# Latents normed inside the attention stage, head weights in fewer pieces, and the squares of x summed in the output projections

## The reference, cut to what matters

```python
def rms_norm(x, w):
    y = x * rsqrt(mean(x * x, axis=-1) + EPS)
    return y * w

# each layer of the first block; the second block opens alike with norm_mix
h = rms_norm(x, norm_w[l]) * (1.0 + scale) + shift
parts = split_in(h @ w_in[l])          # 256 columns cq, 128 ckv, 32 kr, ...
q = rms_norm(cq, q_norm_w) @ w_uq      # 8 heads of 96; then a norm per head, rope on 32
kv = rms_norm(ckv, kv_norm_w) @ w_ukv  # 8 heads of 64 + 64
...
x = x + gate * (y @ w_out[l])
```

## Time and profile before

| | us |
|---|---|
| median of 3 runs | 4379.31 (4378.44 to 4383.56) |
| the profiled execution: its time | 4386.62 |
| its span | 4384.8 |
| TensorE busy | 3901.9 (89%) |
| VectorE busy | 2111.7 (48%) |
| ScalarE busy | 1575.0 (36%) |
| GpSimd busy | 617.0 (14%) |

### The profile page before, as it was taken

How to read it: one execution, slowest core, us unless ns; L and a number is a source line. 1 busy time by engine, 2 the same in 40 slices (tenths; PEclk the granted TensorE clock), 3 DMA queues, 4 the chain that set the end, 5 groups by cost and what they waited for, 6 DMA issues and landing times. The chain is left out here.

```text
span 4384.8 us, 41863 instructions
## 1 busy us (share of the span) xinstructions
PE 3901.9 (89%) x16132; PEld 2780.2 (63%) x16132; DVE 2111.7 (48%) x2657; ACT 1575.0 (36%) x2450; POOL 617.0 (14%) x300
## 2 busy tenths in 40 slices
PE   4899799999899799999876889898999897999996
PEld 1687555558686455567655866576777675666664
DVE  0391366662373366651438423233343226666665
ACT  1412345541322245441452235522221114555552
POOL 0021200002021200001110011022333330111111
PEclk9999889998999799989888989999999997999997
DMA  4211100002211112122112211022233337999985
GB/s 173 77 39 32 36 15 29 29 29 91 68 44 41 31 53 63 58 80 93 30 20 68 49 40 20 10 72 78 82 94 77 89 121 257 360 352 353 354 293 211
DMA packets 339924, 450.95 MB, mean 103 GB/s; under 512 B 45149, under 2 KB 214418, under 8 KB 338194
## 3 DMA queue, kind: packets, MB, share of 16 engines
q1 hardware_dynamic: 325026, 405.30, 29.5%
q0 software_dynamic: 12112, 25.19, 1.6%
q10 hardware_dynamic: 2592, 17.83, 1.0%
HBM read 408.41 MB, written 59.24 MB: 107 GB/s over the span
## 5 line engine op out<-in xcount | busy, mean ns | idle before, releaser
L1140 PE MATMUL values<-probs,vp 128*128 128x512 f32 x672 | 349.0, 601 | 12.0 <-issue 6.4
L1228 ACT ACTIVATE probs<-scores 128x512 f32<-128x512 f32 (+1 forms) x336 | 196.0, 583 | 307.9 <-PE scores L220 306.2
L218 PE MATMUL scores<-q_hi,k_rest 97*128 97x512 f32 (+1 forms) x336 | 262.4, 781 | 0.0
L3555 PE MATMUL dp<-h_t,abt 128*128 128x512 f32 x544 | 241.9, 597 | 1.1 <-ACT abt L3604 0.9
L3586 ACT ACTIVATE expert_hi<-wu 128x1024 fp32r<-128x1024 f32 x136 | 144.8, 1065 | 250.6 <-PE gp L220 250.6
L1309 DVE TENSOR_REDUCE mx<-made 128x1 f32<-128x640 f32 (+1 forms) x272 | 203.9, 794 | 28.7 <-PE made L1081 27.9
L218 PE MATMUL gates_ps<-x_t_r,ring_r 128*128 128x512 f32 (+1 forms) x560 | 206.2, 368 | 2.6 <-PEq L84 2.6
L218 PE MATMUL smb<-x_t_r,merge_w_r 128*128 128x512 f32 x480 | 195.9, 408 | 13.9 <-POOL merge_w_r L2802 11.1
L730 DVE SCALAR_TENSOR_TENSOR conv_out<-conv_in,vectors,conv_out 128x1295 f32<-128x1295 f32 (+1 forms) x120 | 205.5, 1713 | 4.3
L219 PE MATMUL gates_ps<-h_t_r,ring_hi 128*128 128x512 f32 (+1 forms) x560 | 206.1, 368 | 0.0
L220 PE MATMUL gates_ps<-x_t_r,ring_hi 128*128 128x512 f32 (+1 forms) x560 | 206.0, 368 | 0.0
(11 more groups left out here) (572 smaller groups left out, 9525.9 us busy)
## 6 DMA issues: line engine op xcount, KB each, us to landing
wg<-in_w_gate SPq DMA_DIRECT2D x34, 2048.0 KB, 10.0
wu<-in_w_up SPq DMA_DIRECT2D x34, 2048.0 KB, 11.2
h_t<-in_w_down SPq DMA_DIRECT2D x34, 2048.0 KB, 9.7
ahead_w<-in_w_ada SPq DMA_DIRECT2D x48, 512.0 KB, 3.9
ring_w<-in_w_in SPq DMA_DIRECT2D x44, 512.0 KB, 4.1
mod_w<-in_w_mod ACTq DMA_DIRECT2D x8, 1536.0 KB, 29.2
ahead_w<-in_w_mod SPq DMA_DIRECT2D x24, 512.0 KB, 3.5
out_w<-in_w_out SPq DMA_DIRECT2D x24, 512.0 KB, 4.9
```

The costliest lines, as they stand in the source:

```text
L218: nc.tensor.matmul(out, lhs[1], rhs[0], start=start, stop=False, **kw)
L1140: nc.tensor.matmul(O[b % 2][:, 0:w], vp[g // 2 % 2][:, kb, g % 2 * VD:g % 2 * VD + P], pr[m % 3][:, 0:w], start=kb == 0, stop=kb == nk - 1 ...
L1228: nc.scalar.activation(pr[m % 3][:, 0:w], S[m % 2][:, 0:w], ACT.Exp, scale=scale).then_inc(s.exped, 1)
L3555: m = nc.tensor.matmul(dp[half][:, :], at[:, j, :], wd[u][:, j, half * 512:(half + 1) * 512], start=j == 0, stop=j == FK - 1)
```

## The change

Three things.

1. *Latents.* `latent_norms` is gone. Inside `attention`, the six items (five in layer 1, which has no context queries) follow the order of `made`. Items 0 and 1 are squared, summed, rooted and scaled ahead of the rope of the keys; item n + 2 in step n of head 0. The spread kr goes to other PSUM banks. Scratch lies in the place of x.
2. *Head weights.* Two DMAs for the query weights in place of six, and first in SP's list; GpSimd copies the exchanged rope columns, ahead of its fills, once the DMAs have landed.
3. *Squares.* In both of the first block's output projections ScalarE squares every finished tile of x and VectorE adds the squares over chunks into one tile `summed`, one tile behind its residual. The next wide norm (layer 1, and the delta stage) needs one ones-product per block, and takes all roots at its beginning. The first pair of its weight halves is loaded, rounded and split in the output projection. Layer 0's own wide norm stays.

The core of the diff:

```diff
 def norm_steps(...):
     def sums(pe, i, j):
+        if summed is not None:
+            if j == 0:
+                nc.tensor.matmul(ps[i % 2][:, 0:w], k.ones[:, :], summed[:, t0:t0 + w], start=True, stop=True)
+                    .then_inc(s.summed, 1)
+            return
...
-        for j in range(DK):
-            square(0, j)
-        round_half(nc, ring, act, 0)
+        if summed is None:
+            for j in range(DK):
+                square(0, j)
+        if fresh:
+            round_half(nc, ring, act, 0)
         take_root(0)
-        round_half(nc, ring, act, 1)
+        if summed is not None:
+            for i in range(1, len(blocks)):
+                take_root(i)
...
 def attention(...):
         @block.sync
+            for c in range(2):
+                sp.dma_start(wq[:, c, :, 0:QK], w_uq[:, c, :, :]).then_inc(s.q_in, 16)
+            sp.dma_start(table[NOPE:P, :], a.rope[NOPE:P, :]).then_inc(s.rope_in, 16)
             sp.dma_start(wkv[:, :, :], ...).then_inc(s.k_in, 16)
-            sp.dma_start(table[NOPE:P, :], a.rope[NOPE:P, :]).then_inc(s.rope_in, 16)
-                for c in range(2):
-                    sp.dma_start(wq[:, c, :, 0:QK], w_uq[:, c, :, :]).then_inc(s.q_in, 16)
-                    sp.dma_start(wq[:, c, :, QK:QK + half], w_uq[:, c, :, NOPE + half:QK]).then_inc(s.q_in, 16)
-                    sp.dma_start(wq[:, c, :, QK + half:P], w_uq[:, c, :, NOPE:NOPE + half]).then_inc(s.q_in, 16)
         @block.gpsimd
+            pool.wait_ge(s.q_in, 32)
+            for c in range(2):
+                for to, at in ((QK, NOPE + half), (QK + half, NOPE)):
+                    nc.gpsimd.tensor_scalar(wq[:, c, :, to:to + half], wq[:, c, :, at:at + half], 1.0, None, ALU.mult)
+                        .then_inc(s.turned_q, 1)
         @block.tensor                      # project(g, i)
+                if g == 0:
+                    pe.wait_ge(s.normed, normed_by[i + 1])
+                if g == 0 and kind == "k":
+                    pe.wait_ge(s.k_in, 16)
+                    pe.wait_ge(s.kr_squared, 3)
+                    pe.wait_ge(s.krope_made, 3)
...
+            for i in range(2):
+                sum_latent(i)
             for n in range(NI):
+                if n + 2 < NB:
+                    sum_latent(n + 2)
                 prepare(0, n)
         @block.vector
+            def scale_latent(i):
+                dve.wait_ge(s.lat_rooted, i + 1)
+                for ap, weight in latent(i)[0]:
+                    nc.vector.scalar_tensor_tensor(ap, ap, weight, lat_root[i % 2][:, 0:made[i][2]], ALU.mult, ALU.mult)
+                        .then_inc(s.normed, 1)
+            for i in range(2):
+                scale_latent(i)
...                                        # the rope of the keys
             for n in range(NI):
+                if n + 2 < NB:
+                    scale_latent(n + 2)
                 prepare(0, n)
...
 def project_residual(...):
+                    act.wait_ge(s.added, n + 1)
+                    to = total_sq[:, t0:t0 + w_] if n < nb else sq[n % 2][:, 0:w_]
+                    nc.scalar.activation(to, k.x[:, 2 * g + c, t0:t0 + w_], ACT.Square).then_inc(s.squared, 1)
...
+            def add_square(n):
+                dve.wait_ge(s.squared, n + 1)
+                nc.vector.tensor_tensor(total, total, sq[n % 2][:, 0:w_], ALU.add).then_inc(s.totalled, 1)
...
                     nc.vector.scalar_tensor_tensor(x, ps[t][:, 0:w_], mod[:, gate_at + n, which:which + 1], x, ...)
+                    if ahead and g * per + t > nb:
+                        add_square(g * per + t - 1)
+            if ahead:
+                add_square(n_pairs * per - 1)
```

More of the change, by code:

```diff
@@ L276, in norm_steps @@
     last = len(blocks) - 1
+    summed, fresh = norm.summed, ring.halves == 0
+    sums_each = 1 if summed is not None else DK
     def store(sp):
@@ L365, in norm_tiles @@
 def norm_tiles(nc, es, norm):
-    sq = norm.squares or [es.enter_context(sbuf(nc, f"rm_sq{i}", [P, 512], F32)) for i in range(4)]
-    lg = es.enter_context(sbuf(nc, "rm_log", [P, 512], F32))
-    root = [es.enter_context(sbuf(nc, f"rm_root{i}", [P, 512], F32)) for i in range(2)]
+    sq = norm.squares
+    if norm.summed is None:
+        lg = es.enter_context(sbuf(nc, "rm_log", [P, 512], F32))
+        root = [es.enter_context(sbuf(nc, f"rm_root{i}", [P, 512], F32)) for i in range(2)]
+    else:
+        lg, whole = None, es.enter_context(sbuf(nc, "rm_roots", [P, T1], F32))
+        root = [whole[:, t0:t0 + w] for t0, w, _ in norm.blocks]
     ps = [es.enter_context(psum(nc, f"rm_ps{i}", [P, 512], F32)) for i in range(2)]
@@ L433, in beside_norm @@
             def beside_norm():
-                for j in range(DK):
-                    steps.sums(pe, 0, j)
+                for i in range(1 if norm.summed is None else len(norm.blocks)):
+                    for j in range(DK):
+                        steps.sums(pe, i, j)
                 for i, (t0, w, _) in enumerate(norm.blocks):
@@ L438, in beside_norm @@
                     for j in range(DK):
-                        if i + 1 < len(norm.blocks) and j < DK // 2:
+                        if norm.summed is None and i + 1 < len(norm.blocks) and j < DK // 2:
                             steps.sums(pe, i + 1, 2 * j)
@@ L862, in latents @@
                                       (1, lambda p: cols_of(w_in, C_CKV, p), evac_kv)], blocks, extra=extra)
[L865 to L869, removed]
-    norm_groups(nc, k, items)
 def norm_groups(nc, k, items):
@@ L1006, in attention, with latent @@
         ONCE = 9
+        kr_out = (O[0], O[1], J[:, 2, :])
+        half = ROPE // 2
+        def latent(i):
+            kind, t0, w = made[i]
+            if kind == "q":
+                return [(cq[:, c, t0:t0 + w], col(k, f"q_norm{l}", c)) for c in range(2)], 1.0 / Q_RANK
+            return [(ckv[:, t0:t0 + w], col(k, f"kv_norm{l}"))], 1.0 / KV_RANK
         def squares_of(i):
@@ L1398, in project_residual @@
     total = T1 - first
[L1399 removed]
+    names = "w_in0 w_in1 w_in2 w_in3 x_in0 x_in1 x_in2 x_in3 rounded rest w_rounded w_rest split products added summed biased squared totalled"
     with ExitStack() as es, stage(nc, names) as s, nc.Block() as block:
@@ L1410, in project_residual @@
         early = DK // 2
+        if ahead:
+            ring, ring_columns, total_sq = ahead
+            sq = [es.enter_context(sbuf(nc, f"{name}_sq{i}", [P, 512], F32)) for i in range(2)]
+            assert nc.sbuf_base <= SUMMED_AT and SUMMED_AT + 4 * T1 <= nc.sbuf_top
         def place(g, c):
@@ L1430, in _ @@
                 sp.dma_start(k.x[:, pair, first:T1], kept[:, pair, first:T1]).then_inc(x_in[g], 16)
+            if ahead:
+                for n in range(2):
+                    load_half(sp, ring, n, ring_columns)
         @block.gpsimd
@@ L1442, in _ @@
                                             ALU.subtract).then_inc(s.split, 1)
+            if ahead:
+                for n in range(2):
+                    rest_half(nc, ring, pool, n)
         @block.tensor
@@ L1681, in sum_squares @@
                 last.then_inc(s.qk_summed, 1)
-            for j in range(DK):
-                first.sums(pe, 0, j)
+            for i in range(len(X_NORMS)):
+                first.sums(pe, i, 0)
             for i, (t0, w, _) in enumerate(X_NORMS):
```

162 lines of the change are left out of this document (112 added, 50 removed).

## The result

The changed kernel ("after" below) takes 4332.09 us (median of four runs, 4328.47 to 4333.65), against 4381.44 for the kernel before on the same chip (4378.44 to 4385.11). The ratio is 0.9886, with a 95% interval of 0.9869 to 0.9903: 43 to 57 us faster.

What follows compares the result with a forecast made beforehand. TensorE was busy 89% of the span, so only its idle or starved stretches could yield. 15.1 + 18.4 + 16.1 - 2.8 = 46.8 us off: 4339.8 against the profiled execution, 4332.5 against the median; range 4322 to 4343.

Steps and rivals of the forecast that it cites:

- Copies and their wait: Attention start: GpSimd waits for weights until 6.8 us, then four copies of 128 elements take 1.8, to 8.6.
- rival (c): Attention: copies take 3.44 us each, delaying fills that then hold the first rests; 4 us a layer, 4340; chance 0.06.
- VectorE held by fills: Attention: six GpSimd fills hold six VectorE two-SBUF-input operations; first query from 30.0, its last scaling ends at 33.7 us.
- rival (a): Attention: VectorE is not held by fills, or slips in between; 23.4 us more saved, 4309; chance 0.14.
- Two such operations in a row do not slip in between: Attention: each of two adjacent VectorE two-SBUF-input operations waits out a GpSimd fill, so six operations for six fills.
- The pair on L3003: Evidence from the trace before: two adjacent VectorE operations took 7.89 us beside GpSimd's work, 1.28 without.
- Layer 1's opening: Wide norm of layer 1's convolution: first product at 10.1, second weight pair at 43.3 against 61.7; 18.4 us saved.
- Delta stage: Wide norm opening the delta stage: store lands at 10.0, second weight pair at 49.0 against 65.1; 16.1 us saved.
- Rival (b): Openings: stores of x stay late although the weights are gone; 2.7 and 7 us come back, 4342; chance 0.10.
- Output projections: Both projections' tails: the last tile's square and addition come behind the last residual, 1.4 us each, 2.8 lost.
- Rival (d): Output projections: added sums, held by GpSimd's weight splitting, take part in the pace; 123 us lost, 4453; chance 0.03.
- Rival (e): Both openings: the next weight pair, not the norm, sets them; about 35 us given back, 4367; chance 0.05.

Runs made afterwards that it cites:

- `latents_alone`: The kernel before with only the new attention stage (latents normed inside it, two weight pieces, copies on GpSimd): 4362.79 us, ratio 0.9953.
- `weights_not_ahead`: The changed kernel, with the first pair of weight halves loaded, rounded and split at the next stage's opening again, ahead of x's store: 4348.07 us.

## Why the prediction was right, and where its sum was off

The time (4332.5 forecast, 4332.1 measured) is nearer than its terms were, and that is luck: it came from the reference that the sum was set against. The steps gave 46.8 off the profiled execution; the spans gave 53.0. The profiled execution before was 7.3 above its median, that after only 1.6 above its own (4333.65 and 4332.09), and the 5.7 between them about cancel the 6 us that the sum lacked. Point by point:

- **Copies and their wait.** Forecast from 6.8 to 8.6, measured 6.7 to 8.75 (four in 2.04). Right; rival (c) is out. The range of 0.1 to 3.44 each was wide, the tenth of a fill plus a start was the right neighbour.
- **VectorE held by fills.** The mechanism stands: without SBUF reads the gain is another 22 us (rival (a)'s 4309, reached at 4310 once its condition is made true). The size was off in its parts. "Two such operations in a row do not slip in between" is the step that did not hold: of each adjacent pair one waited and one passed (3.48 and 0.74), while I counted six holds of 3.53. That the fills grew to 3.98, and that the first item's pair was held too, makes up for most of it, so the end of the first query's last scaling was off by only 1.6 (32.1 for 33.7). A further 1.1 is the cost of the remaining latents: forecast 0.7 lost, but from that end to head 0's last rest it takes 17.3 us after and 17.7 before, so they are fully covered. Attention: 10.1 and 10.7 by `latents_alone`, for 7.4 and 7.7. The pair on L3003 was read rightly, as two holds of some 4 us each, beside GpSimd operations no longer than the fills; but it is no rule for every pair. Its second operation starts at 3007.88, behind GpSimd's at 3007.49, where the passing scalings start ahead of the next fill.
- The Trainium skill, "SBUF — State Buffer", section "Who interferes with whom", has a GpSimd instruction that reads SBUF contend with a two-input VectorE instruction and one that only writes not. The trace agrees with both halves: 3.89 for two scalings beside fills, 1.15 for the same two beside memsets. My prediction used the first half and did not ask what the second offered. It also told the rule as one-sided, VectorE waiting; in the same section the order of issue decides which engine waits. The starts given here (504.97 before 505.03, 505.62 behind it, 3007.88 behind 3007.49) agree, though no run varied that order by itself.
- **Layer 1's opening.** Forecast 18.4, measured 17.7. The rounding that waits for the store began at 7.4 (8.4), first product at 8.9 (10.1), VectorE's end at 38.6 (38.5), second pair at 44.0 (43.3). The 2.7 us taken for the weights were right (10.0 to 7.4 from issue to landing); the other 1.0 is that the store is now issued at the stage's start. VectorE's chain started earlier by it and lost that again to ScalarE's roundings, for which it waited 4.4 us.
- **Delta stage.** Forecast 16.1, measured 17.6; the rounding began at 7.4, below my lower bound of 8.4, so leaving layer 1's estimate for 10.0 was the error. The load at the end is as said (35.7 for 37.2, and a wait of 7.71 where 7.65 had been seen). Rival (b), late stores, is what `weights_not_ahead` brings back; with the weights away it does not occur.
- **Output projections.** Forecast 1.4 each, measured 1.45 in the row and +1.5 and +1.1 in the segments. Rival (d) is out by the doubled additions.
- **Rival (e)**, the next weight pair sets the openings: true at the margin in the delta stage (7.71 of waiting), but the load is issued when the first half is used, and that moved with the norm.

The corrected sum: 10.1 + 10.7 + 17.7 + 17.6 - 2.6 = 53.5, for 53.0 in the spans. What stays open: whether the order of starts alone decides which operation of a pair passes, and what moves segment D by up to 10 us between kernels that are the same there.

## What to carry to other kernels

When work moves to where another engine was doing something harmless, list what that something does to the operations now beside it. Here the fills by multiplication cost some 20 us under a busy VectorE, and another operation for the same rows got them back. Under the idle VectorE of before they were cheap, but not free: they held both rope additions (3.42 and 1.87 us for 0.68), and TensorE's first query product waited for the second:

```profile
522.73 3.75 PE L1056 MATMUL made<-cq,wq 128*128 128x512 f32 x4 [11.06 <-DVE krope L1370]
```

What memsets would give the kernel before was not run. The last piece of its weights, issued at 515.33 and some 5 us on its way, cannot have been there before about 520 (an estimate), so it is 2 or 3 us at most in layer 0.

A load that is "hidden" may still delay the transfer behind it in the queue that the path waits for: moving 1 MB of weights away from ahead of the store was worth 3.4 us in one stage and 10.1 in the other. Put a forecast made on one profiled execution against the median only with the difference in sight, since the execution after need not lie above its own median as well.

## What the runs showed of the hardware

- A GpSimd multiplication of 1 x 1280 elements took 3.44 us, a memset of the same row 1.16, on the same partition.
- GpSimd waits too: a fill (3.44) that starts behind a passing VectorE operation took 3.98 us; four copies of 128 x 128 took 2.04 undisturbed, 2.67 and 3.06 beside or after VectorE's scalings.
- ScalarE made the same four copies in 0.89 us:

```profile
503.90 0.89 ACT L1313 ACTIVATE wq<-wq 128x128 f32<-128x128 f32 x4
```

- The same 2 MB store landed after 7.4 us with nothing ahead of it, after 9.9 or 10.0 behind 1 MB of weights of one matrix and after 16.4 or 17.0 behind 1 MB of the wider one.
